# A transformer layer on one core: the order in which SyncE asks for the w_o and w_ada chunks

## The reference

```python
mod = silu(c) @ w_ada + b_ada              # w_ada: 2048 x 12288
sh1, sc1, g1, sh2, sc2, g2 = split(mod, 6)
h = rmsnorm(x, norm1_g) * (1 + sc1) + sh1
q_a, k_a, v_a, q_b, k_b, v_b = split(h @ w_qkv)
y = concat([rmsnorm(sliding_window_attention(...)), rmsnorm(moba_attention(...))]) @ w_o
x = x + g1 * y
h = rmsnorm(x, norm2_g) * (1 + sc2) + sh2
x = x + g2 * hier_moe(h, ...)              # 32 experts, 2 of them for each token
return rmsnorm(x, final_g)
```

## Time and profile before

| | |
|---|---|
| median of 3 runs | 1537.61 us (1537.11 to 1540.99) |
| the profiled execution | 1537.11 us, span of the trace 1535.4 us |
| mean granted TensorE clock | 0.953 of full speed (2.4 GHz) |
| TensorE matmul busy | 1327.3 us, 86% |
| VectorE busy | 659.7 us, 43% |
| DMA | 572.09 MB, mean 373 GB/s |

### The profile page before, as it was taken

The page is one execution under the profiler, slowest core; times in us unless marked ns, Lnnn a source line. Parts: engine busy times, 40 slices in busy tenths (PEclk is TensorE's granted clock), DMA queues, the critical chain, the costliest instruction groups (busy, mean ns, idle before and its releaser), DMA issues.

```text
span 1535.4 us, 14533 instructions
## 1 busy us (share of the span) xinstructions
PE 1327.3 (86%) x5692; PEld 672.2 (44%) x5692; DVE 659.7 (43%) x965; ACT 140.5 (9%) x394; POOL 63.0 (4%) x76
## 2 busy tenths in 40 slices
PE   2799998987996689989889789899899889988885
PEld 2678767766885553323223223233333322332331
DVE  4557785797649331242233232332332233223234
ACT  2120000095000110000000000000000000000002
POOL 2000000013000001000000000000000000000000
PEclk9899999999998789999999999999999999999998
DMA  9999998986889706999999999999999999999991
GB/s 333 397 355 399 400 406 314 338 315 155 338 323 339 325 28 266 424 426 425 426 427 427 426 423 429 425 427 426 427 425 425 429 425 426 428 424 427 426 424 74
DMA packets 96294, 572.09 MB, mean 373 GB/s; under 512 B 6048, under 2 KB 28752, under 8 KB 54400
## 3 DMA queue, kind: packets, MB, share of 16 engines
q1 hardware_dynamic: 94256, 567.64, 90.7%
q0 software_dynamic: 2000, 3.95, 1.0%
HBM read 569.38 MB, written 2.18 MB: 372 GB/s over the span
## 4 chain that ended last, share of the span: by engine, by line
PE 63%; DMA 23%; DVE 8%; issue 3%; ACT 1%; SPq 1%; DVEq 0%; POOL 0%; POOLq 0%; ACTq 0%
PE PS L1337 20%; DMA ring<-in_w_up 20%; PE PS L1358 10%; PE PS L1188 9%; PE PS L1317 8%; PE PS L1262 6%; PE PS L1193 4%; DMA ring<-in_w_ada 3%; DVE W L803 2%; PE PS L1299 2%; DVE W L1073 1%; PE PS L1138 1%; DVE W L774 1%; PE PS L1167 1%; DVE W L893 1%
## 5 line engine op out<-in xcount | busy, mean ns | idle before, releaser
L1337 PE MATMUL PS<-ring,W 128*64 128x512 f32 x1024 | 241.8, 630 | 37.0 <-DMA ring<-in_w_up 36.8
L1358 PE MATMUL PS<-ring,W 128*64 128x512 f32 x1024 | 231.9, 606 | 27.4 <-DVE W L1073 17.6
L1337 PE MATMUL PS<-ring,gysq 128*64 128x512 f32 x1024 | 228.9, 603 | 18.7 <-DMA ring<-in_w_up 15.2
L1188 PE MATMUL PS<-r,ring 128*128 128x256 f32 x768 | 170.2, 384 | 8.3 <-DVE r L813 6.6
L1051 DVE TENSOR_TENSOR r<-r,PS 128x512 f32<-128x512 f32 x128 | 87.9, 687 | 200.7 <-PE PS L1317 200.7
L1337 PEld LDWEIGHTS PS<-ring,W 128*64 128x64 f32 x1024 | 81.6, 145 | 191.6 <-issue 191.6
L1188 PEld LDWEIGHTS PS<-r,ring 128*128 128x128 f32 x768 | 147.8, 193 | 31.4 <-DVE r L813 7.4
L1056 DVE TENSOR_SCALAR W<-W 128x256 f32<-128x256 f32 x32 | 22.0, 689 | 314.0 <-ACT W L702 314.0
L803 DVE SCALAR_TENSOR_TENSOR W<-ring,sm,W 128x2048 f32<-128x2048 f32 x60 | 140.9, 2349 | 35.0 <-DMA ring<-in_w_ada 31.9
L1337 PEld LDWEIGHTS PS<-ring,gysq 128*64 128x64 f32 x1024 | 78.0, 139 | 167.7 <-issue 167.7
L1358 PEld LDWEIGHTS PS<-ring,W 128*64 128x64 f32 x1024 | 75.8, 139 | 162.3 <-issue 142.7
(11 more groups left out here) (213 smaller groups left out, 728.8 us busy)
## 6 DMA issues: line engine op xcount, KB each, us to landing
ring<-in_w_gate SPq DMA_DIRECT2D x64, 2048.0 KB, 25.5
ring<-in_w_up SPq DMA_DIRECT2D x64, 2048.0 KB, 27.1
ring<-in_w_down SPq DMA_DIRECT2D x64, 2048.0 KB, 27.2
ring<-in_w_ada SPq DMA_DIRECT2D x32, 2048.0 KB, 15.0
ring<-in_w_qkv SPq DMA_DIRECT2D x17, 2048.0 KB, 16.5
ring<-in_w_ada SPq DMA_DIRECT2D x32, 1024.0 KB, 14.3
ring<-in_w_o SPq DMA_DIRECT2D x8, 2048.0 KB, 10.2
ring<-u_scr SPq DMA_DIRECT2D x2, 2048.0 KB, 20.4
```

The lines of the kernel that those rows point to most:

```text
L1188: last = mm(ps[:, sub * T:(sub + 1) * T], w[:, t, (2 * b + sub) * P:(2 * b + sub + 1) * P], hT[:, QT * q + t, :], start=(t == 0), stop=(t ...
L1337: last = mm(PS[64 * j:64 * j + 64, i % 2, :].rearrange("p (m n) -> p m n", m=2), hE[i % 2][:, k], w[:, :, t, 256 * j:256 * j + 256], start ...
L1358: last = mm(PS[64 * q:64 * q + 64, 4 + i2, :], hidT[:, b, 64 * j:64 * j + 64], w[:, b, 512 * ch:512 * ch + 512], start=(j + b == 0), stop= ...
```

## The change

Only the order in which `stream_plan` lists the chunks of w_o and the last sixteen chunks of w_ada is changed.

```diff
-    add("wo", 0, "pe", "w")
-    for _ in range(4):
+    for c in range(WO_CHUNKS):
+        add("wo", c, "pe", "w")
         add("adv", next(late), "adv", "a")
-    for c in range(1, 4):
-        add("wo", c, "pe", "w")
-    for c in range(WO_CHUNKS):
-        if c + 4 < WO_CHUNKS:
-            add("wo", c + 4, "pe", "w")
-        for _, item in zip(range(2), late):
-            add("adv", item, "adv", "a")
+        add("adv", next(late), "adv", "a")
```

## The result

| | before | changed |
|---|---|---|
| median of the runs, side by side | 1538.33 us | 1553.49 us |
| ratio | | 1.0092, 95% interval 1.0077 to 1.0107 |
| the profiled execution | 1537.11 us | 1552.62 us |
| span | 1535.4 us | 1550.8 us |
| mean TensorE clock | 0.953 | 0.950 |

The changed kernel is 15.2 us slower, 0.9%. A second comparison, on one chip with e5 to e7, gave 1552.68 against 1538.47 us: 14.2 us, ratio 1.0095 (1.0080 to 1.0111). The forecast was slower, 1546.0 us, 1541 to 1551; the measured time lies above that range.

A forecast was written before the change was run, and what follows sets the result against it. It took column sum 2 with VectorE's rows, then TensorE's pass 7, to bound the stage's end; late W7 (8.4 idle) and clock (2.1) start VectorE's pass 7 8.4 us later: 1537.1 + 8.4, plus 0.5 for the median, 1546.0, range 1541 to 1551.

The forecast's parts named there:

- The rival in which W7 isn't held up: W7 lands 8.1 us after issue, at 475.9; stage only 0.3 us longer, 1538; chance 0.09 (in time or nearly).
- that of a loop that takes it back: Rival: the expert stage's first loads keep their old times, so the delay vanishes, about 1538; chance 0.03.
- Faster by other ways: Rival: A20 to A25 land up to 2 us sooner, at best 3.4 us gained, 1534; chance 0.02 for any way.
- W7 comes 6.0 later: Ring queue ahead of pass 7: W7 lands 6.0 us after A29 (475.9), at 481.9; TensorE idles 8.4 us.
- W7's service: Time the queue spends on W7 behind A29 before pass 7: forecast 6.0 us.
- the upper bound: High case: w_o chunks take 6.7 each, +11.3; with POOL's small transfers adding 2.8 if they hit W7, +14.
- The passes ahead of it: Passes 5 and 6: W5 0.3 late with the pick-up, moving column sum 2 and the rows behind by 0.3.
- The clock: TensorE's pass 7 after its idle time: half speed at first, adding 2.1 us; 0 if the clock held.
- The forecast of no gap for W3 and W4: Passes 3 and 4: W3 lands with 4.2 us to spare, W4 with 2.0, so neither pass waits.
- W6's: Gap ahead of pass 6: W6 lands at 459.7, 1.2 us late, costing nothing by itself.
- the queue becomes the bound of every pass: Rival: service of 6.7 makes passes 5 and 6 wait 2 us each, +11.3 to +14, 1549 to 1551; chance 0.18.
- The Trainium skill's rule on pieces of 512 B and more: Line rate for such pieces: w_o and A chunks both served in 5.0 us, W7 at 480.6, sum +7.0; not followed.

The follow-up runs named there:

- e5: Column sum 2 put behind TensorE's pass 4 in place of pass 5, against the changed kernel: 5.9 us over the kernel before.
- e7: Kernel before with column sum 2 behind pass 4 and VectorE's last four rows moved behind the rescaling, between the transposes' copies: 14.5 us faster than the kernel before.
- e1: The changed order, but with W7 issued ahead of A28 and A29: ratio 0.9994 to the kernel before, no difference.
- e2: The kernel before with only W7 moved, to behind A29: 9.4 us over the kernel before (6.5 to 11.4).
- e3: The changed kernel, but POOL's load of b_ada for G2 issued only when pass 7 is over: 9.0 us over the kernel before.
- e6: The kernel before with column sum 2 behind pass 4 in place of pass 5: 5.5 us faster than the kernel before.
- e4: The changed kernel, but w_o chunks loaded in pieces of 8 KB in place of 1 KB, same 2 MB: 5.9 us over the kernel before.

## Why the prediction was wrong

The chain was right: W7 behind A28 and A29, these behind the G2 rows, these behind column sum 2; a gap ahead of pass 7; VectorE taking up pass 7 late; nothing taken back in the loop (956.8 against 956.6 us). The rival in which W7 isn't held up is out by e1 and e2, that of a loop that takes it back by the last column of the table. Faster by other ways did not happen. What failed is the size: the step "W7 comes 6.0 later" than A29 (it came 10.1 later) and, with less weight, two more terms of the sum; and the range took the worst of them too lightly. By the two profiled executions, VectorE's start of pass 7 moved by 16.3 us where 8.4 were forecast:

- **W7's service, +4.1.** It came 10.1 us after A29, not 6.0, since POOL's load of b_ada was under way. The sum had put that collision at +2.8 and only into the upper bound, because it had been read as hitting A31 in the kernel before. But W7 stands where A30 stood, so it meets POOL's load first. e3 took the load away and W7 took 5.9. The trace of before had the price: A30 and A31, with that load beside them, landed at 483.1 and 491.5, that is 7.5 us after A29 (475.6) and 8.4 after A30, together 5.9 more than twice the 5.0 of the other A chunks. The mean rate of 480 to 488 showed less than half of it.

```profile
L410 SPq DMA_DIRECT2D ring<-in_w_ada x1: 367/367/367, 473.8 to 473.8; - x1
DMA to landing us min/median/max: 9.3/9.3/9.3
...
L410 SPq DMA_DIRECT2D ring<-in_w_ada x1: 367/367/367, 478.7 to 478.7; - x1
DMA to landing us min/median/max: 12.8/12.8/12.8
```

- **The passes ahead of it, +1.8.** W5 was forecast 0.3 late with the pick-up and came 1.85 late, since A21 landed 6.4 us after A20, not 5.0. Column sum 2 and the G2 rows moved by 2.1 us (462.01 against 458.44, less 1.4 of the next term), not 0.3. e1 shows that by itself this costs little; in the changed kernel it delays A28, A29 and W7. In e2, where these passes are in time, the stage is only 1.0 us shorter, as W7 took 10.9 us behind A29 there.
- **Ahead of pass 1, +1.4.** The changed execution was 1.4 us later already at 389.71 (388.28 before), in code and loads that the change hardly touches. Pass 0 starts between 371.9 and 374.4 in the ten traces, and the two latest belong to e1 and e6, of which neither is slower than before; e3 and e5, with the changed order up to there, are the two earliest. So it is no cost of the change; how much of it the medians hold is open.
- **The clock, +0.4.** 2.1 forecast; pass 7 took 16.3 us against 13.8, and 17.1 in e2 with the longest gap.
- **The rest, +0.2:** A28 and A29 took 0.1 to 0.2 us longer each than in the row.

Given back behind the stage: 1.1 us in the trace. The small write of the modulation row to `m_scr`, which stands in the chain there, took 1.4 less, and TensorE's matmuls of line 1293 took 0.25 more (30.60 against 30.35). The write was issued 3.8 us before the last of the ring's loads ahead of the loop landed, where it was 6.9 in the kernel before; that this is why it was shorter is likely, but not shown:

```profile
m_scr<-W POOLq DMA_DIRECT2D x1, 8.0 KB, 4.0
```

It took 5.4 us before. The forecast had put the stretch behind the transposes at no change. So 16.3 - 1.1 + 0.2 in the loop = 15.4 us of span, and the difference of the medians is 15.2 and 14.2.

The forecast of no gap for W3 and W4 was right: neither pass 3 nor pass 4 waits. W6's was 0.70 against 1.2. The rival "the queue becomes the bound of every pass" had a piece of the truth, the later W5, but not its reason: w_o chunks were served in 5.8 to 6.0 us, not 6.7.

Of the 14.9 us that the stage grew by, e1 assigns 12.6 to W7's place (14.9 - 2.3). Of those, e3 assigns 3.6 to POOL's load (14.9 - 11.3), and e5 assigns 6.8 to the wait for column sum 2 (14.9 - 8.1); the two overlap with what is left, since W7, when it lands earlier, also meets other loads.

The Trainium skill's rule on pieces of 512 B and more ("DMA: Bandwidth & Descriptors", section Specifications) was weighed against the rows and set aside. e4 bears the rows out: w_o chunks in 1 KB pieces cost 5.8 to 6.0 us for 2 MB in the changed kernel, in 8 KB pieces 4.9 to 5.1. The same page's section "Queues, rings and completion order" says that a DMA engine takes turns between the queues that have work for it. That agrees with e3: the load of another queue, issued 7 us after W7, delayed it by 4 us although W7 had been issued first.

## What to carry to other kernels

In a queue that waits in order, a load inherits the wait of every load ahead of it; before it is moved behind another, ask what frees that one's slot, and what frees it in turn (here two slots and a column sum on TensorE that looked unrelated). Where a transfer gets a new place in time, see what other queues move then, and carry that as a term of the sum, not as an upper bound. And look first for the wait that sets the end: moving column sum 2 by one pass and four rows behind the transposes gained 14.5 us, where ordering the same loads evenly lost 14 to 15.

## What the runs showed of the hardware

A load of 256 KB on POOL's queue that reads each row 32 times took 4 to 5 us of the ring's time when it met W7 (changed, e2), and two A chunks beside it took 5.9 us more than elsewhere in the kernel before, where 256 KB at the 425 GB/s of a clean stretch would be 0.6 us. DMA share stayed at 1 while the rate fell to 243 GB/s. Whether it is the repeated rows that make it so dear isn't shown: no run loads the same bytes in another form.

TensorE's clock fell to half speed in each of its gaps in this stage from 3.87 us (ahead of e7's transposes, granted clock 0.50 in 492 to 497) to 15.7 us. In the gap ahead of pass 7 it fell too, and came back 3.8 us (e5) to 6.2 us (e2) after the pass had begun, which made a pass of 13.8 us into one of 15.9 to 17.1.
